# Triangular solve of an RWKV-7 chunk on one core: the evacuation of E and D after each doubling level, split between ScalarE and VectorE

## What is computed

```python
def step(S, inp):
    r_t, w_t, k_t, v_t, kk_t, a_t = inp
    sa = jnp.einsum('bhvk,bhk->bhv', S, -kk_t)
    S = (S * w_t[:, :, None, :] + sa[..., None] * (kk_t * a_t)[:, :, None, :]
         + v_t[..., None] * k_t[:, :, None, :])
    return S, jnp.einsum('bhvk,bhk->bhv', S, r_t)
```

## Time and profile before

| what | value |
|---|---|
| median of 3 runs | 1844.28 us (1843.1 to 1844.76) |
| the profiled execution, its own time | 1845.74 us |
| its span, first to last instruction | 1844.0 us |
| PE busy over the span | 95% |
| DVE, ACT, POOL busy | 52%, 22%, 33% |
| mean granted TensorE clock | 0.979 |

### The profile page before, as it was taken

How to read it: one execution, slowest core, us unless ns; L and a number is a source line. 1 busy time by engine, 2 the same in 40 slices (tenths; PEclk the granted TensorE clock), 3 DMA queues, 4 the chain that set the end, 5 groups by cost and what they waited for, 6 DMA issues and landing times.

```text
span 1844.0 us, 34696 instructions
## 1 busy us (share of the span) xinstructions
PE 1749.5 (95%) x14741; PEld 1327.4 (72%) x14741; DVE 959.6 (52%) x1766; ACT 402.3 (22%) x933; POOL 601.8 (33%) x418
## 2 busy tenths in 40 slices
PE   5999999999997886999999999999999999999998
PEld 4566666666665554666666888888888888888887
DVE  2767767767766774665325344434333334535422
ACT  2333333334333233555001110111001000000000
POOL 3563664555455430001200122211222210734332
PEclk9999999999997888999999999999999999999999
DMA  9443344324322006110402011111011111333431
GB/s 367 142 148 106 88 132 139 97 91 152 99 70 73 8 7 174 47 47 1 186 23 94 23 46 46 46 46 34 35 46 46 46 46 64 123 95 115 141 99 55
DMA packets 80431, 159.00 MB, mean 86 GB/s; under 512 B 28731, under 2 KB 57227, under 8 KB 76054
## 3 DMA queue, kind: packets, MB, share of 16 engines
q1 hardware_dynamic: 76262, 115.81, 19.6%
q10 hardware_dynamic: 4016, 40.96, 6.3%
HBM read 128.60 MB, written 20.48 MB: 81 GB/s over the span
## 4 chain that ended last, share of the span: by engine, by line
PE 50%; DVE 1%; issue 0%; ACT 0%; DVEq 0%
PE psum L2333 45%; PE psum L2312 5%; PE psum L2322 0%; DVE u_sum L2559 0%; DVE mixT L2560 0%; DVE u_sum L2564 0%; PE psum L2328 0%; DVE mixT L2543 0%; DVE rb L2576 0%; DVE hid L2540 0%; DVE hid L2539 0%; DVE hid L2535 0%; DVE yout L2676 0%; DVE part L2675 0%; DVE part L2625 0%
## 5 line engine op out<-in xcount | busy, mean ns | idle before, releaser
L2333 PE MATMUL psum<-mixT,wA 128*128 128x264 f32 x1408 | 338.6, 389 | 1.9 <-DVE rb L2576 1.5
L2333 PEld LDWEIGHTS psum<-mixT,wA 128*128 128x128 f32 x1408 | 269.0, 191 | 48.8 <-DVE rb L2576 1.7
L2333 PE MATMUL psum<-u_sum,wA 128*128 128x264 f32 x1232 | 298.7, 388 | 0.5 <-DVE u_sum L2559 0.5
L461 PE MATMUL psum<-wsl,xt 128*128 128x368 f32 (+1 forms) x1092 | 283.1, 449 | 8.3 <-DMA wsl<-in_w_in 5.0
L2333 PEld LDWEIGHTS psum<-u_sum,wA 128*128 128x128 f32 x1232 | 235.4, 191 | 41.6 <-issue 0.9
L461 PEld LDWEIGHTS psum<-wsl,xt 128*128 128x128 f32 (+1 forms) x1092 | 149.6, 171 | 90.8 <-issue 17.4
L2490 POOL TENSOR_TENSOR wA<-wA 128x512 f32<-128x512 f32 x22 | 27.9, 1268 | 427.9 <-DMA wA<-in_w_gate 231.3
L2333 PE MATMUL psum<-hid,wA 128*128 128x264 f32 x528 | 120.2, 386 | 2.1 <-DVE hid L2627 1.5
L2333 PEld LDWEIGHTS psum<-hid,wA 128*128 128x128 f32 x528 | 100.2, 190 | 19.9 <-issue 2.8
L1956 PE MATMUL psum<-kT,qT 104*128 104x346 f32 (+7 forms) x224 | 77.6, 464 | 10.1 <-DMA kT<-scratch_kT 9.4
L1297 POOL TENSOR_TENSOR Ls<-Lraw,con 128x512 f32<-128x512 f32 x45 | 49.1, 1100 | 95.3 <-ACT Lraw L964 65.2
(11 more groups left out here) (351 smaller groups left out, 2840.7 us busy)
## 6 DMA issues: line engine op xcount, KB each, us to landing
wsl<-in_w_in ACTq DMA_DIRECT2D x27, 1472.0 KB, 6.7
wA<-in_w_down SPq DMA_DIRECT2D x32, 704.0 KB, 4.1
wA<-in_w_gate SPq DMA_DIRECT2D x22, 512.0 KB, 4.3
wA<-in_w_up SPq DMA_DIRECT2D x22, 512.0 KB
mixed<-proj SPq DMA_DIRECT2D x8, 784.0 KB
xt<-in_x_tiles SPq DMA_DIRECT2D x9, 512.0 KB, 6.0
wsl<-in_w_in SPq DMA_DIRECT2D x3, 1472.0 KB, 11.5
out_y<-hid SPq DMA_DIRECT2D x1, 4224.0 KB, 13.9
```

The source lines that it names most:

```text
L461: return pe.matmul(out, lhsT, rhs, start=start, stop=stop)
L2333: ins = pe.matmul(pb[bank][:, 0:NW], left(k), right(k), start=first and k == 0, stop=k == depth - 1, skip_group_check=not first)
```

## The change

ACT's `e_out` copies only the first of the two banks at levels 0 to 3. A new DVE function `ed_out` copies the second one, from a place of its own in DVE's list, and raises D_ok; PE's `level_t` and `level_ed` wait for both E_ok and D_ok. Level 4 is as before. D_ok was raised once per tile and is now raised five times, hence the new counts.

```diff
@@ PE
         def level_t(t, i):
             pe.wait_ge(s["Ls_ok"], t * n_lv + i + 1)
             pe.wait_ge(s["E_ok"], t * (n_lv + 1) + i + 1)
+            pe.wait_ge(s["D_ok"], t * n_lv + i + 1)
         def level_ed(t, i):
             pe.wait_ge(s["T1_ok"], t * n_lv + i + 1)
-            if i == 0:
-                pe.wait_ge(s["D_ok"], t + 1)
+            if i:
+                pe.wait_ge(s["D_ok"], t * n_lv + i + 1)
+            else:
+                pe.wait_ge(s["D_ok"], t * n_lv + 1)
@@ ACT
         def e_out(t, i):
             act.wait_ge(s["ED_ps"], t * n_lv + i + 1)
             if i < n_lv - 1:
-                copy(ED[:, :, :, :, :].rearrange("p a k j n -> p a (k j n)"), both).then_inc(s["E_ok"], 1)
+                copy(ED[:, 0].rearrange("p k j n -> p (k j n)"), both[:, 0]).then_inc(s["E_ok"], 1)
@@ DVE
+        def ed_out(t, i):
+            dve.wait_ge(s["ED_ps"], t * n_lv + i + 1)
+            dve.tensor_copy(ED[:, 1].rearrange("p k j n -> p (k j n)"), both[:, 1]).then_inc(s["D_ok"], 1)
@@ DVE, the list of a step
             level_t(t, 0)
             sample_scores(t, 0)
             lat_means(f)
+            ed_out(t, 0)
             if t:
                 y_out(t - 1)
             lats(f)
...
             level_t(t, 1)
             sample_scores(t, 2)
+            ed_out(t, 1)
             mix_lora(f)
...
             level_t(t, 2)
             sample_scores(t, 4)
+            ed_out(t, 2)
             lora_add(f)
...
             level_t(t, 3)
             sample_scores(t, 6)
+            ed_out(t, 3)
             qk_sums(f)
```

More of the change, by code:

```diff
@@ L777, in sample_keys @@
             if k < 2:
-                pe.wait_ge(s["D_ok"], LAST + 1)
+                pe.wait_ge(s["D_ok"], LAST * n_lv + 1)
             else:
@@ L1625, in masks_b @@
             run(tt(Dc[:, 1], four(pb[7][:, 256:]), bcast(c_("first"), 1, 4), ALU.mult))
-            named(tt(Dc, Dc, eye24, ALU.add), "D_ok", f + 1)
+            named(tt(Dc, Dc, eye24, ALU.add), "D_ok", f * n_lv + 1)
         def masks_k(f):
```

## The result

The changed kernel takes 1928.45 us (median of 4 runs, 1923.15 to 1936.66), the kernel before 1844.52 in the same comparison: ratio 1.0459, 95% interval 1.0421 to 1.0497. It is 84 us slower; 1920 was predicted, with 1888 to 1948 as the range. The profiled execution took 1929.19 us, its span is 1927.4.

The account below looks back on a forecast made before the run. PE's own list was taken to set the pace in tiles 0 to 6. Waits of 63.4 us plus 13 of clock gave 76 us on 1845.74: 1922, or 1920 against the median; range 1888 to 1948.

Parts of the forecast that it names:

- the clock: PE's new gaps at levels 0 and 3 lower its granted clock: one gap in two, 2 us a drop, 13 us.
- (a): Level 0: `y_out` starts late behind DVE's copy, so PE stands 2.69 us at L515; 1.7 in tile 7.
- (b): Level 1: `mix_lora` starts late behind the copy, so PE's L532 comes 2.12 us later; 3.4 in tile 7.
- (c): Level 2: the second half of `up` waits 0.42 us for L1515, which stands behind the copy.
- (d): Level 3: `qk_sums` starts late behind the copy, so PE's `level_ed(t, 4)` waits 3.07 us.
- Left out: Behind level 4: DVE ends some 0.6 us later against PE; 0 to 0.3 us more, not counted.
- Tiles 7 and 8: Tile 7 costs 7 us, an estimate; tile 8, with no next tile's work behind the copies, 1 us.
- The signs: Expected profile: tiles 1 to 6 72 to 78 us; PE waits 2.7, 2.1, 3.1; DVE idle 1.8, over 3.
- the clock falls at every long gap: Rival: every long PE gap throttles the clock; 1948 us (1935 to 1955), chance 0.14.
- The partial case: Rival: engines catch up, only the level 0 and 3 waits remain, full clock; 1892 us (1855 to 1906), chance 0.24.
- The copy work that fits into DVE's idle time: Rival: the copy's wait falls into DVE's 19 us of idle time per tile; 1842 us, chance 0.03.

Follow-up runs that it names:

- the filled kernel: Changed kernel with unread matmuls for PE in the three places where it idles 1.8 to 3 us: 1909.21 us, ratio 1.0359.
- the copy's work alone: Kernel before plus a 0.69 us DVE sum over T1s at the change's four places, without the wait for `level_ed`: 1851.88 us, ratio 1.0040.
- the four single levels: Four kernels, each splitting one level only, ACT copying both banks elsewhere, no level 0 D_ok wait: levels 0 to 3 1861.86, 1862.65, 1848.24, 1876.30 us.

## Why the prediction was right, step by step

The sign, the places and the mechanism were right. That the size came so close is in part luck: the sum of the terms was closer than the terms were. Of the prediction's 76 us, the waits of tiles 0 to 6 were 55.4 and measured 57.1 (the filled kernel's 518.1 us against 461.0 before); the clock was 13 and measured 19.6; tile 7 was 7 and measured 7.1; tile 8 was 1 and measured nothing. As told, E and D weren't copied at the same time at levels 1 and 2: in tile 2 ACT's half came 2.6 us behind DVE's both times.

- **(a)**, 2.69 us, measured 1.59. The mechanism is as told, but I carried over 1.56 us for L1678. In the kernel before that operation ran beside POOL's L1297, ahead of DVE's L1680 and `lats`:

```profile
224.65 1.56 DVE L1678 TENSOR_TENSOR yb<-yb,bv 128x512 f32<-128x512 f32 x1
224.57 1.09 POOL L1297 TENSOR_TENSOR Ls<-Lraw,con 128x512 f32<-128x512 f32 x1
```

  Now DVE comes to it after POOL has finished, and it takes 0.69 (the row at 248.37). The delay gave 0.87 us back; the copy's 0.61 in place of 0.72 gave 0.1. The Trainium skill's GPSIMD Engine Reference, section Specifications, says that POOL shares its SBUF interfaces with VectorE and that VectorE instructions with two SBUF inputs contend for them, which L1678 is. The traces agree: with the copy's work alone everything on DVE comes 0.7 us later, and there POOL's operation (229.09 to 230.46) meets the one ahead, `yb<-yb,vec`, which takes 1.47 us in place of 0.69, while `yb<-yb,bv` behind it takes 0.69. So it is the meeting and not the instruction. In the same trace T1s, with one input in PSUM, runs beside the next such POOL operation and takes 0.69.
- **(b), (c), (d)**: 2.12, 0.42, 3.07 us, measured 2.06, 0.58, 3.12.
- **Left out**: 1.03 us per tile behind level 4. About 0.4 of it is the level 0 D_ok wait, which stood in the diff and which I priced at nothing: D of the next tile is finished after E, and `level_t` didn't wait for it before. In tile 8 that wait is 2.85 us. For the rest, 0.6, I had allowed 0 to 0.3; half of it is PE's wait for `state_p`, 1.04 us in the filled kernel's tile 1 against 0.75 before, the other half is open. (a) was too large by 1.1 and this too small by 1.03, so 8.3 us per tile met 8.38 by luck: the two errors have nothing to do with each other.
- **Tiles 7 and 8**: 7 + 1 us; tile 7 took 7.1 more, and from there to the end of the phase nothing is added. That too is luck: 2.85 of it are the D_ok wait at its end, which I hadn't priced. (a), 1.7, measured 1.08 (PE waits 4.87 for `lat` in place of 3.79), (b), 3.4, measured 3.3. With the idle time filled the tile takes 4.6 us more than before, not 7.1.
- **The clock**: 13 us, measured 19 by the filled kernel, and this is the term that was too small: it makes up 6 to 7 of the 8 us between 1920 and 1928. I priced (a) and (d) at one fall in two, 6.5 of 13. In the changed kernel's trace the clock falls behind (a) in 2 of 6 tiles and behind (d) in 5 of 7, 7 of 13, and a fall costs 1.4 us (19.6 over 14), not 2. What I missed is (b): I took 1.9 us of idle time as harmless after one row of the prologue, and behind (b), 1.86 us, the clock falls in all seven tiles. Even the prologue's own row came out the other way in the changed kernel:

```profile
55.96 6.91 PE L461 MATMUL psum<-wsl,xt 128*128 128x368 f32 x16 [1.90 <-ACT proj L967]
```

  The same 16 matmuls behind the same wait took 5.21 us in the kernel before.
- **The signs.** Tiles 1, 3, 4 and 6 are 75.7 to 76.1 us long, but tiles 2 and 5, where the clock falls three times, are 80.0 and so outside the 72 to 78. PE waits 1.83 us for `lat`, not 2.7, so (a) was wrong in size by that sign; 1.86 and 2.97 at the other two places are near the 2.1 and 3.1. DVE's idle time ahead of the copies in tile 2 is 2.2 us at level 0, where 1.8 was named, and 5.0 and 3.1 at levels 1 and 3, over 3 as named.
- **The rivals.** That the clock falls at every long gap is refuted by the 6 of 13 behind which it stays at 1.00. The partial case, where only two waits remain, is refuted by the four single levels, which add up. The copy work that fits into DVE's idle time is the right account for the work, 7 us alone, and for the wait it became true only when the copies were moved. (The times given for the first two of these, 1948 and 1892, were added to the profiled execution and not to the median; on the median they are 1.5 us lower.)

Whether the clock falls behind a wait depends on more than that wait: with level 1 alone split, the same 1.86 us ahead of the lora transposes stand in seven tiles, and the clock stays at 1.00 behind each. What decides it wasn't separated.

## What to carry to other kernels

A wait costs more than the instruction that it guards. Before giving a lightly used engine an operation that waits for the bottleneck, look in its program order at what stands behind it and who needs that soonest: two idle engines that copy at once were worth nothing that shows here, and the copy's place in the list, with the wait that went with it, was worth 84. Place such an operation where its input has just become ready and the work behind it has slack, tile by tile, since the last tile's list may differ. And bound the gain first by the one row that says how long the bottleneck waited for the old operation.

## What the runs showed of the hardware

Idle time of PE under 2 us can cost the clock, and doesn't always; nor does a longer wait. The stretches behind the wait for `lat` in tile 1 (1.83 us, ended at 174.75) and in tile 2 (1.84 us, ended at 250.75), both of the changed kernel:

```profile
174.00:176.00 2.00, 1.25 (x36) 1.02 (x37) 1.76 (x8) 0.49 (x1) 0.00 (x0) 1.00 0.91 283
176.00:178.00 2.00, 2.00 (x10) 1.41 (x10) 0.80 (x2) 0.60 (x1) 1.09 (x1) 1.00 1.01 430
```

```profile
250.00:252.00 2.00, 1.25 (x36) 0.96 (x37) 1.76 (x8) 0.49 (x1) 0.00 (x0) 0.94 1.00 283
252.00:254.00 2.00, 2.00 (x6) 1.49 (x7) 0.81 (x2) 0.60 (x1) 1.09 (x1) 0.50 1.00 418
```

The same instructions and the same wait, once at 2.4 GHz and once at 1.2. During or behind how many of the waits the granted clock fell, in tiles 0 to 6 of one trace each:

| kernel | 1.8 us for `lat` | 1.9 us at the lora transposes | 3.0 us for `T1h` |
|---|---|---|---|
| changed | 2 of 6 | 7 of 7 | 5 of 7 |
| no D_ok wait at level 0 | 2 of 6 | 6 of 7 | 5 of 7 |
| one level split (0, 1, 3) | 2 of 6 | 0 of 7 | 4 of 7 |

The wait alone has shorter ones: behind 1.2 us the clock fell in none of 13, behind 2.35 in 2 of 7. So the wait at the lora transposes cost the clock nearly every time where the others stood near it, and never by itself. That goes with the spread of the whole kernel: its four runs lie 13.5 us apart, at mean clocks of 0.959 to 0.966, the slowest at the lowest, where the kernel before had 2.6 us between its four.
